# Moving two gate projections of a hybrid layer out of the first projection and into the attention stage

## The reference, cut to what matters

```
h = rms_norm(x, norm_pre_w)
proj = h @ w_in                 # 1024 -> 8 groups of 512 columns, and 8 more columns
a_q, a_k, a_v, a_z, d_q, d_k, d_v, d_z, d_b, d_a = split(proj)
moba_out = moba_attention(a_q, a_k, a_v) * silu(a_z)
qkv = silu(causal_depthwise_conv([d_q, d_k, d_v], conv_w))
o = gated_delta_rule(l2norm(g_q), l2norm(g_k), g_v, g, beta)
gdn_out = rms_norm(o) * silu(d_z)
mixed = [moba_out, gdn_out] @ w_out
x = x + rms_norm(mixed, norm_post_w)
```

## Time and profile before

| | |
|---|---|
| median of 3 runs | 2451.68 us (2448.6 to 2452.36) |
| time of the profiled execution | 2451.22 us |
| its span | 2449.5 us |
| last copy of `project_first` starts | 238.05 us |
| first instruction of `attention` | 240.42 us |
| first `score` of `attention`, first half | 245.42 us |
| first `score` of the second half | 300.33 us |
| first work of `delta_prepare` | 357.13 us |

### The profile page before, as it was taken

How to read it: one execution, slowest core, us unless ns; L and a number is a source line. 1 busy time by engine, 2 the same in 40 slices (tenths; PEclk the granted TensorE clock), 3 DMA queues, 4 the chain that set the end, 5 groups by cost and what they waited for, 6 DMA issues and landing times. The chain is left out here.

```text
span 2449.5 us, 36562 instructions
## 1 busy us (share of the span) xinstructions
PE 2191.9 (89%) x11207; PEld 1910.3 (78%) x11207; DVE 1692.2 (69%) x3348; ACT 819.4 (33%) x1405; POOL 770.2 (31%) x677
## 2 busy tenths in 40 slices
PE   3999887854999998797869999999998999999997
PEld 2877567744777776586869999999998788888885
DVE  2474455444768684569758888888876788888886
ACT  2443322123222222322424444444432333333333
POOL 2000004200000000037547878878754222222220
PEclk9999559977999998898989999999999999999998
DMA  4331000020433331420336879878688999999995
GB/s 105 80 88 39 1 0 1 0 66 20 125 100 86 91 87 52 156 76 18 123 121 226 261 259 294 276 251 290 226 274 298 343 338 337 337 339 337 335 339 207
DMA packets 225737, 428.83 MB, mean 175 GB/s; under 512 B 18404, under 2 KB 151684, under 8 KB 225412
## 3 DMA queue, kind: packets, MB, share of 16 engines
q1 hardware_dynamic: 168068, 254.97, 32.9%
q0 software_dynamic: 41472, 151.01, 18.0%
q10 hardware_dynamic: 16128, 22.03, 2.5%
HBM read 381.80 MB, written 46.14 MB: 175 GB/s over the span
## 5 line engine op out<-in xcount | busy, mean ns | idle before, releaser
L2066 PE MATMUL bank<-xt_hi 128*128 128x512 f32 x768 | 302.9, 394 | 8.0 <-DVE xt_lo L1995 8.0
L1786 PE MATMUL bank<-xt_hi,u_hi 128*128 128x384 f32 x896 | 309.5, 345 | 0.0
L1786 PE MATMUL bank<-xt_hi,u_lo 128*128 128x384 f32 x896 | 300.8, 336 | 0.0
L1786 PE MATMUL bank<-xt_lo,u_hi 128*128 128x384 f32 x896 | 300.4, 335 | 0.0
L2066 PE MATMUL bank<-xt_hi,xt_lo 128*128 128x512 f32 x768 | 300.2, 391 | 0.0
L2066 PE MATMUL bank<-xt_lo,xt_hi 128*128 128x512 f32 x768 | 300.1, 391 | 0.0
L1648 POOL DMA_INDIRECT row_slot<-in_peer_v_dram,row_index x128 | 139.0, 1086 | 391.7 <-DVE row_x L1999 373.2
L2042 ACT ACTIVATE xt_hi<-xh 128x1024 fp32r<-128x1024 f32 x128 | 135.8, 1061 | 337.8 <-PE bank L2066 333.6
L1992 DVE TENSOR_TENSOR xt_lo<-xh,xt_hi 128x1024 fp32r<-128x1024 f32 x128 | 156.8, 1225 | 84.0 <-ACT xt_hi L2042 84.0
L1317 POOL TENSOR_TENSOR k_wlo<-k_raw,k_whi 128x2048 fp32r<-128x2048 f32 x4 | 18.4, 4604 | 616.4 <-ACT k_whi L1437 616.4
L1727 POOL TENSOR_TENSOR u_two<-u_match,u_weight_hi 128x512 fp32r<-128x512 f32 x96 | 179.1, 1866 | 97.0 <-DVE u_match L1813 96.6
(11 more groups left out here) (421 smaller groups left out, 4955.6 us busy)
## 6 DMA issues: line engine op xcount, KB each, us to landing
xh<-in_peer_v_dram SPq DMA_DIRECT2D x128, 512.0 KB, 5.4
xh<-in_peer_u_dram SPq DMA_DIRECT2D x113, 512.0 KB, 4.0
x_raw<-in_w_in_dram SPq DMA_DIRECT2D x56, 512.0 KB, 7.1
v_ga<-acts SPq DMA_DIRECT2D x128, 192.0 KB, 5.4
acts<-xh ACTq DMA_DIRECT2D x112, 192.0 KB
p_raw<-in_w_in_dram SPq DMA_DIRECT2D x16, 1024.0 KB, 8.9
weights<-u_spread POOLq DMA_DIRECT2D x32, 512.0 KB, 6.3
v_gg<-weights SPq DMA_DIRECT2D x128, 128.0 KB, 5.2
```

The lines of the kernel that those rows point to most:

```text
L1786: mm = pe.matmul(k.ps[4 + b][:, 0:DENSE], w[b][:, c, :], x[:, c, 0:DENSE], start=(c == 0 and w is uhi and x is hi), stop=(c == DC - 1 and ...
L2066: mm = pe.matmul(k.ps[q][:, :], h[b][:, t * P:(t + 1) * P], v[b][:, f], start=False, stop=False, skip_group_check=True)
```

## The change

The first projection does 24 chunks in 6 steps (`Z_FROM = 24`); its order is d_q, d_k, d_v, a_q, a_k, a_v. The convolution and SiLU of the sixth pair, which lay in step 6, follow the last step. The 8 chunks of `a_z` and `d_z` move into `attention`, which now gets `xt_hi` and `xt_lo`. One chunk belongs to each quarter, with loads of 512 KB into two buffers, a copy on ScalarE (`high`), a subtraction on VectorE (`low`), 24 matmuls into bank 7 and a copy out on ScalarE (`keep_z`). The 24 matmuls go in six groups of four: in steps 1, 2 and 3 of a quarter, one group before `turn` and one before `weigh`. The two halves are written out instead of looped.

```
+Z_FROM = 24
-    steps = PROJ // step
+    steps = Z_FROM // step
-        chunk = lambda i: (i * step + DQ0) % PROJ
+        chunk = lambda i: (i * step + DQ0) % DZ0
-            with eng.Fori(2, 2 + unit_pairs) as i:
+            with eng.Fori(2, steps - 1) as i:
                 body(i, True, True, True)
-            for i in range(2 + unit_pairs, steps):
-                body(i, i <= pairs, False, False)
+            body(steps - 1, True, True, True)
...
+                silu(pairs)
+                convolve(pairs)
...
-def attention(nc, k, proj, mixed):
+def attention(nc, k, io, xt, proj, mixed):
+    z_chunks = [Z0 + c for c in range(4)] + [DZ0 + c for c in range(4)]
+    halves, quarters = A_HEADS // 4, 4
+    z_of = lambda i, q: i * quarters + q
...
+            @block.sync
+            def _(sp):
+                for j, c in enumerate(z_chunks):
+                    if j >= 2:
+                        sp.wait_ge(w_lo[j % 2], after(j // 2))
+                    sp.dma_start(raw[j % 2][:, :, :], w_dram[:, :, c * P:(c + 1) * P]).then_inc(raw_in[j % 2], 16)
...
+                def project(i, n, part):
+                    q, r = n // quarters, n % quarters
+                    if r == 0:
+                        return
+                    j, b = z_of(i, q), z_of(i, q) % 2
+                    if r == 1 and part == 0:
+                        pe.wait_ge(w_lo[b], after(j // 2 + 1))
+                        pe.wait_ge(z_kept, after(j))
+                    at = (r - 1) * 8 + part * 4
+                    for m in range(at, at + 4):
+                        c, (w, x) = m // 3, ((whi, hi), (whi, lo), (wlo, hi))[m % 3]
+                        mm = pe.matmul(k.ps[7][:, :], w[b][:, c, :], x[:, c, :], start=(m == 0), stop=(m == 3 * DC - 1))
+                    if r == quarters - 1 and part == 1:
+                        mm.then_inc(z_product, 1)
...
                         if n + 2 < n_steps:
                             score(i, n + 2)
+                        project(i, n, 0)
                         if n + 1 < n_steps:
                             turn(i, n + 1)
+                        project(i, n, 1)
                         weigh(i, n)
...
+                low(0)
+                for i in range(halves):
...
+                        if n % quarters == 2 and z_of(i, n // quarters) + 1 < len(z_chunks):
+                            low(z_of(i, n // quarters) + 1)
...
+                high(0)
+                for i in range(halves):
                     for n, (p, b, qt) in enumerate(steps):
+                        j = z_of(i, n // quarters)
+                        if n % quarters == 1 and j + 1 < len(z_chunks):
+                            high(j + 1)
...
+                        if n % quarters == 0 and j:
+                            keep_z(j - 1)
                     keep(i, n_steps - 1)
+                keep_z(len(z_chunks) - 1)
```

More of the change, by code:

```diff
@@ L398, in _, with silu @@
                 act.activation(bias[:, 0, :], bias[:, 0, :], ACT.Exp).then_inc(decay_rate, 1)
+                def silu(i):
+                    for h in range(2):
+                        act.wait_ge(acc_done[h], after(i))
+                        act.activation(proj[:, i * 2 + (DQ0 + h - 2), :], acc[h][:, :], ACT.Silu).then_inc(silu_done[h], 1)
                 def body(i, convolved, square, scaled):
@@ L412, in body @@
                     if convolved:
-                        for h in range(2):
-                            act.wait_ge(acc_done[h], after(i))
-                            act.activation(proj[:, i * 2 + (DQ0 + h - 2), :], acc[h][:, :], ACT.Silu).then_inc(silu_done[h], 1)
+                        silu(i)
                     if square:
@@ L434, in low, with convolve @@
                                       ALU.subtract).then_inc(w_lo[b], 1)
+                def convolve(i):
+                    chain = Chain(dve, vec, i - 1, 2 * (G_CONV - 1), done=1)
+                    for h in range(2):
+                        dve.wait_ge(silu_done[h], after(i - 1))
+                        x = lambda upto: proj[:, i * 2 + (DQ0 + h - 2), 0:upto]
+                        tap = lambda j: k.cols[:, bass.ds(i * 2 + (w0 + j * n_ch + h - 2), 1)]
+                        chain(dve.tensor_scalar(acc[h][:, :], x(T), tap(G_CONV - 1), None, ALU.mult))
+                        for j in range(G_CONV - 2, -1, -1):
+                            s = G_CONV - 1 - j
+                            ins = dve.scalar_tensor_tensor(out=acc[h][:, s:T], in0=x(T - s), scalar=tap(j), in1=acc[h][:, s:T],
+                                                           op0=ALU.mult, op1=ALU.add)
+                            if j:
+                                chain(ins)
+                            else:
+                                ins.then_inc(acc_done[h], 1)
+                    chain.end()
                 def body(i, convolved, square, scaled):
@@ L438, in body @@
                     if convolved:
-                        chain = Chain(dve, vec, i - 1, 2 * (G_CONV - 1), done=1)
                         for n in range(step):
                             dve.wait_ge(kept[n], after(i))
[L442 to L455, removed]
+                        convolve(i)
                     if not (isinstance(i, int) and i == steps - 1):
@@ L487, in _ @@
                 body(1, True, True, False)
-                with dve.Fori(2, 2 + unit_pairs) as i:
+                with dve.Fori(2, steps - 1) as i:
                     body(i, True, True, True)
-                for i in range(2 + unit_pairs, steps):
-                    body(i, i <= pairs, False, False)
-def attention(nc, k, proj, mixed):
+                body(steps - 1, True, True, True)
+                convolve(pairs)
+def attention(nc, k, io, xt, proj, mixed):
+    hi, lo = xt
+    w_dram = io["w_in"][0].rearrange("(c p) n -> p c n", p=P)
+    z_chunks = [Z0 + c for c in range(4)] + [DZ0 + c for c in range(4)]
+    halves, quarters = A_HEADS // 4, 4
+    z_of = lambda i, q: i * quarters + q
     with ExitStack() as st:
+        raw, whi, wlo = ([k.sb(f"a_{n}{b}", [P, DC, P], dt, ctx=st) for b in range(2)]
+                         for n, dt in (("raw", F32), ("whi", F32R), ("wlo", F32R)))
+        raw_in, w_hi, w_lo = (k.sems(f"a_{n}", 2) for n in ("raw_in", "w_hi", "w_lo"))
+        z_product, z_kept = k.sem("a_z_product"), k.sem("a_z_kept")
         vtok = k.sb("a_vtok", [P, TT, A_HEADS * A_DH], ctx=st)
@@ L563, in weigh @@
                     mm.then_inc(weighted, 1)
-                with pe.Fori(0, A_HEADS // 4) as i:
+                def project(i, n, part):
[13 more added lines that the diff above has]
+                for i in range(halves):
                     score(i, 0)
@@ L595, in normalise, with low @@
                                       stat[:, 3, n:n + 1], None, ALU.mult).then_inc(normed, 1)
-                with dve.Fori(0, A_HEADS // 4) as i:
+                def low(j):
+                    dve.wait_ge(w_hi[j % 2], after(j // 2 + 1))
+                    dve.tensor_tensor(wlo[j % 2][:, :, :], raw[j % 2][:, :, :], whi[j % 2][:, :, :].bitcast(F32), ALU.subtract
+                                      ).then_inc(w_lo[j % 2], 1)
+                low(0)
+                for i in range(halves):
                     chain = Chain(dve, vec, i, 2 * n_steps, done=1)
@@ L627, in keep, with high, keep_z @@
                     act.activation(probs_t[:, n % 2, 0:w], k.ps[2 + n % 2][:, 0:w], ACT.Copy).then_inc(kept_t, 1)
-                with act.Fori(0, A_HEADS // 4) as i:
+                def high(j):
+                    act.wait_ge(raw_in[j % 2], after(j // 2 * 16 + 16))
+                    if j >= 2:
+                        act.wait_ge(z_product, after(j - 1))
+                    act.activation(whi[j % 2][:, :, :], raw[j % 2][:, :, :], ACT.Copy).then_inc(w_hi[j % 2], 1)
+                def keep_z(j):
+                    act.wait_ge(z_product, after(j + 1))
+                    act.activation(proj[:, z_chunks[j], :], k.ps[7][:, :], ACT.Copy).then_inc(z_kept, 1)
+                high(0)
+                for i in range(halves):
                     for n, (p, b, qt) in enumerate(steps):
+                        j = z_of(i, n // quarters)
+                        if n % quarters == 1 and j + 1 < len(z_chunks):
+                            high(j + 1)
                         w = (qt + 1) * P
@@ L2120, in build @@
                 k.end_stage()
-            attention(nc, k, proj, mixed)
-            k.end_stage()
+                attention(nc, k, io, xt, proj, mixed)
+                k.end_stage()
             o = mixed[:, :, A_HEADS * A_DH:D]
```

## The result

| | runs | median | range | ratio to before, 95% |
|---|---|---|---|---|
| before | 4 | 2451.72 us | 2448.6 to 2452.36 | |
| after | 4 | 2428.55 us | 2424.74 to 2433.4 | 0.9911 [0.9896, 0.9926] |

The kernel is faster by 23 us, 0.9%. The forecast was 2425 us, 2411 to 2447. The profiled execution is the slowest of its four (2433.4 us, span 2431.6), so I read stages, and use its total with care. The stages compare as follows (times of before from the earlier trace rows and the table ahead of them).

What follows compares the result with a forecast made beforehand. TensorE was taken to bound the attention, at 1.2 GHz. Removed work less the tail (-35.3), start-up (+3.2), quarters (+2.6), cold stretches (+5.0) and table load (-1.3) gave -25.8 us from 2451.2: 2425 us, range 2411 to 2447.

Steps and rivals of the forecast that it cites:

- attention from first `score` to `delta_prepare`: Attention after its start-up: 2.6 us for longer quarters, 5.0 for cold stretches, less 1.3 for a table load.
- Removed and exposed: End of first projection: removing steps 6 and 7 gains 43.4 us, an exposed VectorE tail gives back 8.1.
- the sum: Whole kernel: -35.3 + 3.2 + 2.6 + 5.0 - 1.3 = -25.8 us.
- Start-up: Start of attention: first `score` waits for a new load, `high` and `low`; 3.2 us more, between 2.2 and 5.4.
- The clock: Attention: the new matmuls lift TensorE from 1.2 to 2.4 GHz, at 0.226 us each instead of 0.43.
- The first rival: Attention: the clock stays low, quarters hold 22.6 us of TensorE work, +49 us, 2500 us in all; chance 0.12.
- The quarters: Attention: a new quarter takes 11.88 + 1.0 = 12.9 us, 0.33 more than before; 2.6 us for eight.
- Cold stretches: Start of each attention half: TensorE at the lower clock until it rises, 2 to 2.5 us each; 5 us together.
- The swinging clock: Attention: the clock falls at step 0 of every quarter, costing 20 us in place of 5; 2440 us; chance 0.10.
- The chain takes the new work whole: Attention: `high`, `low` and `keep_z` delay the softmax chain 2.9 us a quarter, 23 us in all; 2446 us; chance 0.12.
- One table load: Attention: with the halves written out, the table load before the first exponential occurs once instead of twice; 1.3 us less.

Runs made afterwards that it cites:

- rerun: The changed kernel run again, unchanged: 2427.15 us, ratio 0.9911 to the kernel before.
- early convolution: Changed kernel with the sixth convolution ahead of the last scaling and both last SiLUs ahead of the last bank copies: 2417.25 us, ratio 0.9873.
- prefetch: Changed kernel with the first chunk's weights loaded, copied and subtracted inside the first projection: 2419.79 us, ratio 0.9881.
- kernel with six matmuls a quarter: Kernel before plus 6 unread matmuls in each quarter of the attention, first projection as before: 2466.61 us, ratio 1.0067.
- late `high`: Changed kernel with ScalarE's copy of the next chunk's weights behind the exponential and keep of step 1: 2423.45 us, ratio 0.9897.
- fillers: Kernel before plus unread matmuls in each quarter of the attention: 2456.77 us with 24, 2437.96 us with 12, 2466.61 us with 6.
- fillers of twelve: Kernel before plus 12 unread matmuls in each quarter of the attention, two in each of six places: 2437.96 us, ratio 0.9945.

## Why the prediction was right, point by point

| step of the prediction | forecast | first profile | profile of the rerun |
|---|---|---|---|
| start of the stage's last copy, 192 matmuls of 0.226 us removed | -43.4 | -45.5 | -45.4 |
| tail behind the last copy | +8.1 | +8.2 | +8.2 |
| barrier behind the tail, longer than before | none | +0.3 | +0.3 |
| start-up of the attention | +3.2 (2.2 to 5.4) | +6.3 | +6.9 |
| attention from first `score` to `delta_prepare` | +6.3 | +7.4 | +5.6 |
| gained at `delta_prepare` | 25.8 | 23.3 | 24.5 |

*Removed and exposed.* Right. The tail's last piece was forecast at 8.1 us behind the last copy and is 8.2. The copy came 2.1 us earlier than forecast, and 1.9 of these are the scatter at `p_ba_t` (52.22 against 54.08; 52.38 in the rerun). Counted from that copy, the gains at `delta_prepare` are 21.4 and 22.8 us, where the medians give 23.2 and 22.6. Against the 25.8 of the sum about 3 us are missing, and the start-up is where they went. That this tail sets the end of the stage, and is not hidden, the early convolution confirms: moving it forward brought 7.7 us at the start of the attention and 9.9 in the medians.

*Start-up.* The mechanism was right (`low(0)` ahead of the copies of q and k, behind a load issued only then); its term was mis-sized, and outside the bounds that I gave. The load took 8.2 us to its first reader, 8.7 in the rerun. What follows the load took 3.14 us where the rows gave 3.09 (1.06 + 1.23 + 0.80), so the whole miss of 3.1 us is the load. (My pieces add up to 7.0 and 10.2 us, not to the 7.2 and 10.4 that I wrote.) I took a value near the 3.89 us of the earlier trace rows since "only two loads are in flight"; the median of 7.1 us was nearer, and even that is too low. The transfer rate is the visible difference, as the windows above show. Why a load with one neighbour in its queue is slower than one that other loads follow, no run tells apart. The prefetch shows what the load, `high` and `low` cost together: 6.1 to 6.6 us at the first `score`, 7.4 in the medians.

*The clock.* It rose, as forecast, and this decides the change. The first rival (2500 us) is refuted by the clock of 1.00 and by quarters of 12.9 us. But the reasons that I gave for it don't hold, so the hit on this term is in part luck. I argued from a packed run of 18 us without a hole. The kernel with six matmuls a quarter has such a run (15.00 of 15.00 us) and stays at 0.50, and the kernel before with 98% did too. So missing holes alone don't lift the clock. Twelve matmuls a quarter do; what decides between six and twelve, these runs don't settle. My argument against the rival, that much of the time would be "the very matmuls that run at the upper clock in the first projection", fits the runs with 0, 6, 12 and 24 of them better, but it too is only an argument.

I also argued from one rise behind 16 transposes. The same trace has the same 16 transposes 8.4 us before, with no rise behind them, and elsewhere 32 transposes with a rise:
```profile
495.40:499.20 3.80, 3.65 (x16) 3.28 (x16) 2.47 (x4) 3.70 (x6) 0.00 (x0) 0.50 0.03 4
499.20:503.90 4.70, 0.00 (x0) 0.00 (x0) 4.38 (x23) 4.67 (x9) 0.00 (x0) 0.50 0.00 0
598.20:603.20 5.00, 5.00 (x24) 5.00 (x25) 2.83 (x4) 3.19 (x5) 0.00 (x0) 0.50 0.00 0
603.20:606.00 2.80, 1.26 (x10) 1.02 (x8) 2.60 (x5) 2.08 (x4) 0.00 (x0) 0.95 0.00 0
```
The attention of the changed kernel opens with 16 transposes too (3.65 busy us from 203.47). Behind them the clock stays at 0.50 in the first profile, and in the rerun it is 1.00 from 207 to 209. So such a run can be followed by a rise and needn't be, even with the same instructions, and my rows were one case of several. The Trainium skill (TensorE: Matmul & The Clock Gate, Part 4: PE-mode transpose), which I set aside on those rows, holds that transposes don't count as busy in the same way. The rises with nothing but transposes ahead of them (507.9, 603.2, 207 in the rerun) disagree with it. The run with six doesn't decide: transposes are 3.0 of the 15.0 busy us of its quarter.

*The quarters.* 12.9 us forecast, 12.89 and 12.85 measured, with 0.44 us of hole at step 0 where I had 1.0; TensorE's work was 12.45 instead of 11.88, because its own part at the upper clock is not 6.45 us but 12.38 - 24 x 0.22 = 7.1. Two errors of 0.6 that cancel, which is luck. The late `high` proves the place of the hole: 12.36 us without it.

*Cold stretches.* Forecast 5.0 us in two halves. With 2.6 for the quarters as forecast and 2.6 for the table loads as measured (below), 7.4 us are left for them in the first profile (7.4 - 2.6 + 2.6) and 5.6 in the rerun. The clock rose 11.7 us after the first `score`, and some 10 us after it fell at the change of halves. The swinging clock came once, from 294 to 298, behind a step 0; in the rerun it did not come at all. As a steady pattern, 20 us, it is refuted. The Trainium skill (TensorE: Matmul & The Clock Gate, A second HAM failure mode: psum-queue depth-cycling) warns of that; here a hole of 0.44 us in a quarter left the clock at 1.00 in both steady quarters shown, and one dip followed such a hole. The first half took 57.8 us, 2.9 more than before (54.9), the second 61.3 against 56.8.

*The chain takes the new work whole.* Refuted: with the matmuls a quarter is 12.89 us and TensorE has a hole of 0.44 in it, which goes when `high` moves; the chain isn't the bound. Without the matmuls a quarter grows from 12.55 to 12.99 us, not by 2.9, and that growth is the matmul that stays.

*One table load.* One row at L697, as forecast, but the term was half of what it should be. Before, both loads (247.33 and 302.23) stood between the maximum and the exponential, 1.28 us of the chain each. The one that is left ends at 214.00, ahead of the first `score`. So 2.6 us went, not 1.3.

*Where the gain comes from.* The moved matmuls are not hidden in the attention. They cost their full 0.22 us there, as the fillers show, as much as they did in the first projection. What pays is the clock: it shortens TensorE's own work in a quarter from 12.26 to 7.1 us, 5.2 us, about as much as 24 matmuls cost (5.2 us). The fillers of twelve got a part of this gain with no move at all.

## What to carry to other kernels

Where a stage runs at the lower clock, ask first what moved matmuls do to the clock and then what they cost. Here a quarter of 12.55 us took in 24 dense matmuls and grew by 0.34. Matmuls that nobody reads, put in the same places, are a cheap test of this before the move is written. Work that hid a tail, or a first load, exposes it when it goes: here these two together (8.2 and 6.3 us) were nearly two thirds as large as the net gain, and each could be had back by doing the work earlier. A copy for the next chunk was better placed behind the exponential in the queue than ahead of it. And of a pattern in a trace, such as a rise of the clock, look up every case and not one.

## What was unexpected of the hardware

- Six unread matmuls of 512 columns a quarter cost 17 us in the whole and leave the clock at 0.50; twelve save 12 us and bring 1.00; 24 cost 7 us. The time is not monotone in the work.
- TensorE busy for 15.00 of 15.00 us at 0.50: a busy engine does not show that the clock will rise.
- A clock lifted ahead of the first `score` (1.00 from 214 to 218) was at 0.50 again from 220 to 222.
- A load of 512 KB took 8.2 and 8.7 us to its first reader with one more in its queue, against 3.89 for one that other loads followed.
- Behind 16 transposes with nothing else the clock rose at 507.9 and not at 499.2 in the trace of before; behind the 16 at the start of the attention it rose in one of the two profiles of the changed kernel.
